# Convolution FFNs: activations multiplied by the root ahead of the product, and 512-column products from the fifth step on

## What is computed

```python
def rmsnorm(x, g):
    xf = x.astype(jnp.float32)
    y = xf * lax.rsqrt(jnp.mean(xf * xf, axis=-1, keepdims=True) + EPS)
    return (y * g.astype(jnp.float32)).astype(x.dtype)
...
def conv_gated_ffn(h, w_up, conv_w, conv_b, w_down):
    u = h @ w_up                       # 1024 x 5504
    u = lax.conv_general_dilated(u, conv_w...) + conv_b    # depthwise, 3 taps, causal
    gate, val = jnp.split(u, 2, axis=-1)
    return (jax.nn.silu(gate) * val) @ w_down
...
h = rmsnorm(x, ffn_norm[layer])
x = x + conv_gated_ffn(h, ...)
```

## Time and profile before

| | |
|---|---|
| median of 3 runs | 1768.0 us (1767.75 to 1768.23) |
| the profiled execution's own time | 1768.03 us |
| its span, first to last instruction | 1766.3 us |
| PE busy, share of the span | 1754.9 us, 99% |
| PE weight loads | 1688.8 us, 96% |
| DVE busy | 1277.0 us, 72% |
| ACT busy | 1027.7 us, 58% |
| share of PE in the chain that ended last | 93% |

### The profile page before, as it was taken

How to read it: one execution, slowest core, us unless ns; L and a number is a source line. 1 busy time by engine, 2 the same in 40 slices (tenths; PEclk the granted TensorE clock), 3 DMA queues, 4 the chain that set the end, 5 groups by cost and what they waited for, 6 DMA issues and landing times.

```text
span 1766.3 us, 34785 instructions
## 1 busy us (share of the span) xinstructions
PE 1754.9 (99%) x13798; PEld 1688.8 (96%) x13798; DVE 1277.0 (72%) x1859; ACT 1027.7 (58%) x1538; POOL 97.6 (6%) x144
## 2 busy tenths in 40 slices
PE   9999999999999999999999999999999999999998
PEld 8999999999999999999999999999999999998887
DVE  7667868877787886787876687788666776556665
ACT  5776555666555566655566755566444655456444
POOL 3000000122000013000000000002000020000000
PEclk9999999999999999999999999999999999999999
DMA  9445654534565544565554456556555554435652
GB/s 305 148 144 163 198 189 156 189 124 142 170 211 179 184 161 155 168 215 178 169 189 143 144 174 206 181 171 209 171 189 193 164 168 135 165 122 190 196 182 95
DMA packets 238486, 306.32 MB, mean 173 GB/s; under 512 B 13762, under 2 KB 212980, under 8 KB 238332
## 3 DMA queue, kind: packets, MB, share of 16 engines
q1 hardware_dynamic: 236708, 300.27, 52.4%
q0 software_dynamic: 1552, 4.28, 0.7%
q10 hardware_dynamic: 104, 0.07, 0.0%
HBM read 303.53 MB, written 1.07 MB: 172 GB/s over the span
## 4 chain that ended last, share of the span: by engine, by line
PE 93%; DVE 3%; ACT 2%; issue 1%; DMA 1%; DVEq 0%; POOL 0%; ACTq 0%; POOLq 0%
PE ps L1085 26%; PE ps L1086 25%; PE ps L1087 25%; PE ps L1437 7%; PE ps L1439 3%; PE ps L1252 1%; ACT sb_w_hi L887 1%; DVE sb_w_lo L1651 1%; DMA sb_raw<-in_da_w_qkv 1%; PE ps L1272 1%; PE ps L1593 0%; PE ps L1302 0%; PE ps L1289 0%; PE ps L1244 0%; PE ps L1098 0%
## 5 line engine op out<-in xcount | busy, mean ns | idle before, releaser
L1651 DVE TENSOR_TENSOR sb_w_lo<-sb_raw,sb_w_hi 128x2048 fp32r<-128x2048 f32 x283 | 646.6, 2290 | 285.6 <-ACT sb_w_hi L887 285.0
L1085 PE MATMUL ps<-sb_a_hl,sb_w_hi 128*128 128x256 f32 x2608 | 746.9, 286 | 1.5 <-DVE sb_a_hl L1665 0.5
L1086 PE MATMUL ps<-sb_a_hl,sb_w_hi 128*128 128x256 f32 x2608 | 737.7, 283 | 0.0
L1087 PE MATMUL ps<-sb_a_hl,sb_w_lo 128*128 128x256 f32 x2608 | 737.6, 283 | 0.0
L887 ACT ACTIVATE sb_w_hi<-sb_raw 128x2048 fp32r<-128x2048 f32 x283 | 538.5, 1907 | 185.5 <-PE ps L1087 119.4
L1085 PEld LDWEIGHTS ps<-sb_a_hl,sb_w_hi 128*128 128x128 f32 x2608 | 499.6, 192 | 10.1 <-issue 6.5
L1086 PEld LDWEIGHTS ps<-sb_a_hl,sb_w_hi 128*128 128x128 f32 x2608 | 499.8, 192 | 0.4
L1087 PEld LDWEIGHTS ps<-sb_a_hl,sb_w_lo 128*128 128x128 f32 x2608 | 499.7, 192 | 0.0
L1085 PE MATMUL ps<-sb_hh,sb_w_hi 128*128 128x256 f32 x912 | 257.0, 282 | 0.0
L1086 PE MATMUL ps<-sb_hl,sb_w_hi 128*128 128x256 f32 x912 | 256.8, 282 | 0.0
L1087 PE MATMUL ps<-sb_hh,sb_w_lo 128*128 128x256 f32 x912 | 256.6, 281 | 0.0
(11 more groups left out here) (261 smaller groups left out, 1819.6 us busy)
## 6 DMA issues: line engine op xcount, KB each, us to landing
sb_raw<-in_ffn_w_up SPq DMA_DIRECT2D x102, 1024.0 KB, 5.4
sb_raw<-in_ffn_w_down SPq DMA_DIRECT2D x66, 1024.0 KB, 5.0
sb_raw<-in_da_w_qkv SPq DMA_DIRECT2D x23, 1024.0 KB, 5.4
sb_raw<-in_ffn_w_gate SPq DMA_DIRECT2D x22, 1024.0 KB, 5.3
sb_raw<-in_w_o SPq DMA_DIRECT2D x16, 1024.0 KB, 4.9
sb_raw<-in_sb_w_qkv SPq DMA_DIRECT2D x12, 1024.0 KB, 5.2
sb_raw<-in_xa_wkv SPq DMA_DIRECT2D x8, 1024.0 KB, 5.7
sb_raw<-in_w_in SPq DMA_DIRECT2D x8, 1024.0 KB, 5.8
```

The costliest lines, as they stand in the source:

```text
L1085: pe.matmul(o, hi1, hi2, start=start, stop=False, skip_group_check=True)
L1086: pe.matmul(o, hi1, lo2, start=False, stop=False, skip_group_check=True)
L1087: return pe.matmul(o, lo1, hi2, start=False, stop=stop, skip_group_check=True)
L1651: dve.tensor_tensor(w_lo[:, a % RING, :], raw[:, a % RING, :], w_hi[:, a % RING, :].bitcast(F32), ALU.subtract).then_inc(lo_ready, 1)
```

## The change

The six steps 4 to 9 of each of the four convolution FFNs take the wide form. Their activations must then be multiplied by the root already, since `take` no longer multiplies by it: DVE forms x times gain times root in `kT` (`normal_x`, four operations of 256 columns in step 1 and four in step 2), ACT rounds it into the high half of `a_hl[1]` (`normal_hi`, 1024 columns in step 2 and in step 3), DVE subtracts for the low half (`normal_lo`, 1024 columns in step 2 and in step 3), and PE waits for the second `norm_lo` before its loop. In the wide steps ACT has `copy_low` twice, and `take` adds in place of multiplying. PE's loop is as before; the loops of DVE, ACT and SP become three rounds with two steps, with steps 2 and 3 written out ahead of them, in the gated FFNs too.

```diff
--- before.py
+++ after.py
@@ -31,8 +31,8 @@
 DEPTH = 4
 F1, F2 = 2752, 2816
 NSTEP = 11
-NLOOP, LSTEPS = 2, 4
-PE_NLOOP, PE_LSTEPS = 3, 2
+NLOOP, LSTEPS = 3, 2
+NORM_FROM = 4
 NCH = 2 * NSTEP
 HD = 64
 N_BUCKETS, MAX_DIST = 32, 128
...
@@ -70,9 +70,14 @@
     return 0.8 - 0.6 * math.exp(-0.3 * layer)
 
 
+def first_wide(ph):
+
+    return 2 if ph["gated"] else NORM_FROM
+
+
 def plan():
 
-    c = dict(n=0, u=0, f=0, stat=0, sqs=0, scaled=0, tree=0, x=4, hd=0, sg=0, rg=0, tk=0, us=0, mix=0, fill=[0, 0])
+    c = dict(n=0, u=0, f=0, stat=0, sqs=0, scaled=0, tree=0, x=4, hd=0, sg=0, rg=0, tk=0, us=0, low=0, mix=0, fill=[0, 0])
     out = []
 
     def stat(ph):
...
@@ -450,7 +460,11 @@
 
         def wide(ph, s0):
 
-            return ph["wide"] and 2 <= s0 < NSTEP - 1
+            return first_wide(ph) <= s0 < NSTEP - 1
+
+        def normal(ph, s0):
+
+            return wide(ph, s0) and not ph["gated"]
 
         def wide_parts(ph, c, e):
 
...
@@ -470,10 +484,13 @@
 
             up(0, 0)
             up(1, 0)
+            for d in range(2):
+                up(d + 2, 0)
+                down(d, 0)
             with eng.Fori(0, NLOOP) as i:
                 for d in range(LSTEPS):
-                    up(d + 2, LSTEPS * i)
-                    down(d, LSTEPS * i)
+                    up(d + 4, LSTEPS * i)
+                    down(d + 2, LSTEPS * i)
             up(NSTEP - 1, 0)
             for s in range(NSTEP - 3, NSTEP):
                 down(s, 0)
...
@@ -1034,6 +1048,16 @@
                             act.wait_ge(u_free, ph["u"] + 2 * s0 + c - 1 + 2 * s)
                             act.activation(u_low[:, c, :, :], wide_parts(ph, c, 1), ACT.Copy).then_inc(low_copied, 1)
 
+                        def normal_hi(half):
+
+                            cs = slice(4 * half, 4 * half + 4)
+                            act.wait_ge(norm_ready, 2 * ph["index"] + half + 1)
+                            act.activation(a_hi[1][:, cs, :], kT[:, cs, :], ACT.Copy).then_inc(norm_hi, 1)
+
+                        if s0 == 2 and not ph["gated"]:
+                            normal_hi(0)
+                        if s0 == 3 and not ph["gated"]:
+                            normal_hi(1)
                         copy_low(0)
                         newest_tap(0)
                         split(b + (3 if packed(ph, s0) else 4), s)
...
@@ -1433,10 +1457,10 @@
                     u, wl, cs = ph["u"] + 2 * s0 + c, weights(up_block(ph, s0, part), KC), slice(c * P, (c + 1) * P)
 
                     if wide(ph, s0):
-                        o = PS[:, wide_bank(ph, part, c), :]
-                        pe.matmul(o.rearrange("p (e t) -> p e t", e=2), wl[0][:, k, cs], a_hl[a][:, :, k, :], start=k == 0,
+                        o, of = PS[:, wide_bank(ph, part, c), :], 1 if normal(ph, s0) else a
+                        pe.matmul(o.rearrange("p (e t) -> p e t", e=2), wl[0][:, k, cs], a_hl[of][:, :, k, :], start=k == 0,
                                   stop=False, skip_group_check=True)
-                        return pe.matmul(o[:, T:2 * T], wl[1][:, k, cs], a_hi[a][:, k, :], start=False, stop=k == KC - 1,
+                        return pe.matmul(o[:, T:2 * T], wl[1][:, k, cs], a_hi[of][:, k, :], start=False, stop=k == KC - 1,
                                          skip_group_check=True)
                     return product(UB[u % 4][:, part * T:(part + 1) * T], wl[0][:, k, cs], wl[1][:, k, cs],
                                    a_hi[a][:, k, :], a_lo[a][:, k, :], k == 0 and part == 0, k == KC - 1)
...
@@ -1470,7 +1494,7 @@
                             u = ph["u"] + 2 * s0 + c
                             if wide(ph, s0) and s0 == 2 and k == 0:
                                 pe.wait_ge(u_free, u - 3 + max(part, c) + part * c)
-                            elif wide(ph, s0 - 1) and part == 0 and k == 0:
+                            elif (wide(ph, s0) or wide(ph, s0 - 1)) and part == 0 and k == 0:
                                 pe.wait_ge(u_free, u - 1 + 2 * s)
                             elif part == 0 and k == 0 and u >= 4:
                                 pe.wait_ge(u_free, u - 3 + 2 * s)
...
@@ -1555,10 +1579,12 @@
                 first_down = False
                 up(3, 0)
                 down(1, 0)
-                with pe.Fori(0, PE_NLOOP) as i:
-                    for d in range(PE_LSTEPS):
-                        up(d + 4, PE_LSTEPS * i)
-                        down(d + 2, PE_LSTEPS * i)
+                if not ph["gated"]:
+                    pe.wait_ge(norm_lo, 2 * ph["index"] + 2)
+                with pe.Fori(0, NLOOP) as i:
+                    for d in range(LSTEPS):
+                        up(d + 4, LSTEPS * i)
+                        down(d + 2, LSTEPS * i)
                 if packed(ph, NSTEP - 1):
                     packed_up(NSTEP - 1)
                 else:
...
@@ -2037,9 +2063,11 @@
                             ins.then_inc(u_free, 1)
                             return
                         if wide(ph, s0):
-                            dve.wait_ge(low_copied, ph["us"] + 2 * (s0 - 2) + c + 1 + 2 * s)
+                            dve.wait_ge(low_copied, ph["low"] + 2 * (s0 - first_wide(ph)) + c + 1 + 2 * s)
                             dve.tensor_tensor(us[:, c, :, :], wide_parts(ph, c, 0), u_low[:, c, :, :], ALU.add)\
                                 .then_inc(u_free, 1)
+                            if normal(ph, s0):
+                                return
                             dve.wait_ge(u_free, u + 1 + 2 * s)
                             dve.tensor_tensor(us[:, c, :, :], us[:, c, :, :], both(r_all[:, 0, :]), ALU.mult)\
                                 .then_inc(us_ready, 1)
...
@@ -2062,14 +2090,33 @@
                                     scalar=cw[ps, bass.ds(at + rw + 64 * s, 1)], in1=acc[ps, c, h, sh:T],
                                     op0=ALU.mult, op1=ALU.add).then_inc(done, 1)
 
+                    def normal_x(half):
+
+                        for c in range(4 * half, 4 * half + 4):
+                            ins = dve.scalar_tensor_tensor(out=kT[:, c, :], in0=x[:, c, :],
+                                                           scalar=gains[:, c, G_FFN + ph["conv"]:G_FFN + ph["conv"] + 1],
+                                                           in1=r_all[:, 0, :], op0=ALU.mult, op1=ALU.mult)
+                        ins.then_inc(norm_ready, 1)
+
+                    def normal_lo(half):
+
+                        cs = slice(4 * half, 4 * half + 4)
+                        dve.wait_ge(norm_hi, 2 * ph["index"] + half + 1)
+                        dve.tensor_tensor(a_lo[1][:, cs, :], kT[:, cs, :], a_hi[1][:, cs, :].bitcast(F32), ALU.subtract)\
+                            .then_inc(norm_lo, 1)
+
                     if packed(ph, s0):
                         hidden_lo(s0 - 1, s)
+                    if s0 in (1, 2) and not ph["gated"]:
+                        normal_x(s0 - 1)
                     take(0)
                     if s0 and not packed(ph, s0):
                         hidden_lo(s0 - 1, s)
                     older_taps(0)
                     take(1)
                     split(b + (3 if packed(ph, s0) else 4), s)
+                    if s0 in (2, 3) and not ph["gated"]:
+                        normal_lo(s0 - 2)
                     older_taps(1)
                     for c in range(2):
                         f, ps = ph["f"] + 2 * s0 + c, rows(ph, s0, c)
```

More of the change, by code:

```diff
@@ L124, in ffn @@
         ph = dict(kind="ffn", bias_used=c["sg"], index=c["hd"] // NSTEP, F=F, act=0, fill=c["fill"][0] - 1, n=c["n"],
-                  u=c["u"], f=c["f"], hd=c["hd"], up=wup, down=wdown, conv=conv, dst=dst, stat=stat, x=c["x"], wide=conv is None, us=c["us"])
+                  u=c["u"], f=c["f"], hd=c["hd"], up=wup, down=wdown, conv=conv, dst=dst, stat=stat, x=c["x"], gated=conv is None, us=c["us"],
+                  low=c["low"])
         if conv == DEPTH - 1:
@@ L134, in ffn @@
         c["hd"] += NSTEP
-        c["us"] += 2 * (NSTEP - 3) if ph["wide"] else 0
+        c["us"] += 2 * (NSTEP - 3) if ph["gated"] else 0
+        c["low"] += 2 * (NSTEP - 1 - first_wide(ph))
         c["x"] += 4 if dst == "x" else 0
@@ L309, in model_kernel @@
         low_copied = sem("low_copied")
+        norm_ready = sem("norm_ready")
+        norm_hi = sem("norm_hi")
+        norm_lo = sem("norm_lo")
         x_ready = sem("x_ready")
@@ L1011, in newest_tap @@
                             f = ph["f"] + 2 * s0 + c
-                            if wide(ph, s0):
-                                act.wait_ge(us_ready, ph["us"] + 2 * (s0 - 2) + c + 1 + 2 * s)
-                            else:
-                                act.wait_ge(u_free, u + 1 + 2 * s)
+                            act.wait_ge(u_free, u + 1 + 2 * s)
                             if f >= 2:
@@ L1492, in packed_up @@
                         wait_block(pe, b)
-                        pe.wait_ge(u_free, u - (1 if ph["wide"] else 3))
```

(1 more changed line is left out.)

## The result

The changed kernel takes 1797.32 us (median of 4 runs, 1795.65 to 1800.81) against 1768.08 us before: a ratio of 1.0168, 95% interval 1.0156 to 1.018. It is 29.2 us slower, where 21.3 were forecast. The profiled execution took 1795.65 us and has a span of 1793.9 us.

A forecast was written before the change was run, and what follows sets the result against it. PE was taken to bound the kernel, busy 99% of the span. To 1768.03 us it added 27.2 us of waits and 2.4 for starting again, less 8.3 gained: 1789.3 us, range 1783 to 1798.

The forecast's parts named there:

- a clock below full speed behind the longest wait: Sign at PE's wait for the second `norm_lo`: the prediction is wrong if the clock isn't at full speed behind it.
- The lateness: PE's three waits up to up(4), for operations added to DVE in steps 1 to 3: 6.8 us per FFN, 27.2 in four.
- starting again: PE after each of 12 new waits: between nothing and 0.4 us each, 2.4 us in all.
- The gain: 24 ups made wide on PE: 0.35 us each, 8.3 us in all, between 5.3 and 9.8.
- The small fixed cost per matmul: Rival: each matmul saved on PE gives only 2.5 ns, 1.9 us in all, so 1795.7 us; chance 0.06.
- the 4.3 us left in the middle of the loop: Time left before PE's next up needs `take(1)`: ACT's added copies in the wide steps therefore cost nothing.
- The clock: Rival: PE falls to half speed for 4 to 7 us after the longest wait, +8 to +14 us; chance 0.1.
- The idle time absorbs the additions: Rival: DVE's idle time before first splits of steps 2 and 3 takes up 4.6 us per FFN; 1767 us; chance 0.04.
- The late take: Rival: ACT's late copies make PE wait in the 24 wide steps, up to 1 us each, up to 1813; chance 0.04.
- ACT's rounding of 1024 columns: Added to ACT in steps 2 and 3: near 1.0 us each, inside idle time before the newest tap, costing nothing.

The follow-up runs named there:

- e2: The changed kernel with narrow products on unmultiplied activations in the convolution FFNs; multiplied ones still formed and PE still waits for them: 1802.97 us.
- e4: The changed kernel, wide from step 4, but DVE multiplies by the root behind the take and nothing is prepared in steps 1 to 3: 1787.4 us.
- e7: The changed kernel with ACT's next split ahead of its silus and roundings in the convolution FFNs: 1764.77 us.
- e11: e7 with DVE's subtraction for the multiplied activations (`normal_lo`) ahead of the second split of its step: 1758.29 us.
- e9: The changed kernel with 7 and 13 matmuls that serve nothing in PE's two longest waits of each convolution FFN: 1793.5 us.
- e3: As e2, but PE doesn't wait for the multiplied activations, which nothing reads: 1786.73 us.
- e6: The changed kernel with the products of x, gain and root formed on GpSimd in place of DVE: 1798.99 us.

## Why the prediction was right, and where its sum was off

The mechanism that the sum rests on was right, and so was its largest term. That the time lies in the range is in part luck: 1797.32 is 0.7 us under its upper end. The sum lacked one term of 4.8 us and had put another, of 3.8 us, into a rival, and both came on the same side. By one of its own signs the prediction was wrong: it named a clock below full speed behind the longest wait, and 192 to 195 us reads 0.50.

**The lateness** was forecast as 6.8 us per FFN and 0.6 for starting again; 7.25 were measured between down(0) and up(4): in the first FFN 1.07, 1.98 and 3.53 us of idle time and 0.7 for starting again. Four times it is 29.0 against 29.6. DVE's steps 1 and 2 are longer by 1.58 and 2.31 us, as reckoned. That the preparation makes the lateness, and not the wide products, is shown from both sides: e2 has it without them, and e4 has them without it and is on time. That it acts through the chain of DVE and ACT, e7 and e11 show by shortening the chain, with the preparation left in.

**The gain** was forecast as 8.3 us. Free of the clock, the wide steps gain 2.42 us in the third FFN, and 2.17 in the second, where its first two took 16.88 and 17.06 us and the others 16.79: some 9.2 in four (8.9 in e9). The rows of the gated FFN were the right price. The small fixed cost per matmul that the Trainium skill (TensorE: Matmul & The Clock Gate, Back-to-back issue gap) gives was not: that rival is refuted. The estimate from that figure was 1.9 us in all. Which of the two lengths a wide up takes stays open.

**The ends of the FFNs** are the term that the sum lacked: about 1.2 us each in the first three, and as much behind the fourth, 4.8 in all. I had costed the wide steps at nothing on the strength of the 4.3 us left in the middle of the loop. They are left there, but not at the end, where the last hidden values' low halves follow without a down in between. In the kernel before DVE's timeline has them ready, at 307.58 + 0.75, and PE's has down(10) starting at 308.81, only 0.48 us later:

```profile
307.58 0.75 DVE L2094 TENSOR_TENSOR sb_hl<-sb_work,sb_hh 128x256 fp32r<-128x256 f32 x2
```

```profile
308.81 0.28 PE L1085 MATMUL ps<-sb_hh,sb_w_hi 128*128 128x256 f32 x1
```

With the wide steps DVE's lead over PE is smaller. Its second take in step 9 starts 3.81 us ahead of PE's up(10) before (288.78), and 2.61 us ahead of it in the changed kernel (294.44); the timelines of DVE, before and after:

```profile
284.97 0.68 DVE L2047 TENSOR_TENSOR sb_work<-ps,sb_r_all 128x512 f32<-128x512 f32 x1
```

```profile
291.83 0.69 DVE L2067 TENSOR_TENSOR sb_work<-ps,sb_work 128x512 f32<-128x512 f32 x1 [0.90 <-ACT sb_work L1049]
```

These 1.2 us are more than the lead of 0.48. PE's timeline of the changed kernel at its down(10) and at the next phase:

```profile
315.01 0.36 PE L1109 MATMUL ps<-sb_hh,sb_w_hi 128*128 128x256 f32 x1 [0.38 <-DVE sb_hl L2141]
...
321.46 0.36 PE L1109 MATMUL ps<-sb_a_hl,sb_w_hi 128*128 128x256 f32 x1 [0.52 <-ACT sb_a_hl L951]
```

Half of the gain was handed back there. e2, which has no wide products, has no such wait, and e7 and e11, which have them and the earlier splits, have none either. Whether the copies ahead of the take or PE's shorter steps make the 1.2 us, no run tells apart.

**The clock** was a rival with a chance of 0.1, at 8 to 14 us. It happened in every FFN, but cost 3.8 us by the median (e9). My argument against it, that the shorter waits don't add to the longest, is the one that failed: in e3 the clock fell with no wait over 1.99 us. Its price was too high for two reasons. No row stood behind the 4 to 7 us of half speed that it assumed, and a fall lasted 3.4 us, which costs 1.7; and in the profiled execution three of the five falls lie under a wait that hides them. With 29.0 - 9.2 + 4.8 + 3.8 = 28.4 us the measured 29.2 are accounted for but for 0.8.

**The idle time absorbs the additions:** refuted; DVE's 2.29 and 2.32 us stood as before. The reason given, ACT's split queued behind its wait for DVE, was the lever of e7. **The late take** didn't happen in the changed kernel; in e4 its relative did, a period longer than PE's.

ACT's rounding of 1024 columns took 1.04 us in the idle time, as forecast; 3.60 and 2.42 us of it were still left in front of the newest taps.

## What to carry to other kernels

Before work is put on an engine that doesn't bound the kernel, look at whether it is behind at that place: compare when its results are ready with when they are wanted, and count idle time as room only if what ends it doesn't depend on that engine itself. When the bounding engine's step gets shorter, compare the others' period per step with the new one, and look at the last step for itself, where the lead is smallest. If two engines hand work to each other in a ring, the order in each queue may be worth more than the work: here one split per step moved forward turned +29 us into -3, and with one subtraction moved as well -10.

## What was not expected of the hardware

The granted clock fell to half for 3.4 us with no wait over 1.99 us before it and 6 us of full work between the two waits (e3, and the changed kernel's second and third FFN). In e3's first and third FFN waits of nearly the same lengths brought no fall, so no rule can be read from these runs. Two operations of GpSimd with two operands each made four taps of DVE 2.7 times as long (4.78 against 1.76 us, e6): each of the first two taps ended only when one of GpSimd's had.
